# Hybrid MoBA and gated DeltaNet layer: softmax weights of seven heads transposed by DMA as 16-bit halves, their product with V moved to a slot of the delta branch

## The reference

```python
h = rms_norm(x, norm_gain)
aq, ak, av, az, bqkv, bz, bbeta, balpha, gate_a, gate_b = split(h @ w_in)
# branch A, per head; 256 tokens are one block, so attention is causal over all of them
lo = (q * dh**-0.5) @ k.T - slope * distance       # causal, -inf above the diagonal
p = softmax(lo)
ya = (p @ v) * silu(az)
# branch B, per head: causal convolution, then the chunked gated delta rule
tmat = triangular_solve(eye + lower, eye)
u, w = tmat @ vb, tmat @ (kb * exp(g))
out, state = scan over chunks
yb = rms_norm(out) * silu(bz)
merged = sigmoid(gate_a) * (ya @ w_branch_a) + sigmoid(gate_b) * (yb @ w_branch_b)
x = rms_norm(x + merged @ w_out)
```

## Time and profile before

| | |
|---|---|
| median of 3 runs | 771.9 us (771.65 to 772.05) |
| profiled execution, own time | 772.16 us |
| its span, first to last instruction | 770.4 us |
| mean granted clock of TensorE | 0.997 of 2.4 GHz |
| PE busy | 758.4 us (98%) |
| DVE busy | 564.8 us (73%) |
| ACT busy | 464.9 us (60%) |
| POOL busy | 122.1 us (16%) |
| DMA, share of 16 engines | 74.0% |

### The profile page before, as it was taken

How to read it: one execution, slowest core, us unless ns; L and a number is a source line. 1 busy time by engine, 2 the same in 40 slices (tenths; PEclk the granted TensorE clock), 3 DMA queues, 4 the chain that set the end, 5 groups by cost and what they waited for, 6 DMA issues and landing times.

```text
span 770.4 us, 10402 instructions
## 1 busy us (share of the span) xinstructions
PE 758.4 (98%) x3483; PEld 625.7 (81%) x3483; DVE 564.8 (73%) x1265; ACT 464.9 (60%) x697; POOL 122.1 (16%) x179
## 2 busy tenths in 40 slices
PE   8999999999999999999999999999999999999995
PEld 6888888888888888888888888888888888887884
DVE  5769847975895689479758956894798476966563
ACT  5686647656765675476657657764856663535441
POOL 6112011110101021101111120201021002512120
PEclk9999999999999999999999999999999999999998
DMA  9968767886788786778866786778676586798643
GB/s 254 241 170 219 205 163 214 193 217 179 184 209 198 192 208 181 199 192 197 212 174 203 200 217 170 203 188 215 174 213 182 181 222 182 217 331 268 190 153 109
DMA packets 225572, 154.44 MB, mean 200 GB/s; under 512 B 55408, under 2 KB 190576, under 8 KB 225392
## 3 DMA queue, kind: packets, MB, share of 16 engines
q1 hardware_dynamic: 225376, 153.53, 74.0%
q10 hardware_dynamic: 144, 0.26, 0.1%
HBM read 140.64 MB, written 2.11 MB: 185 GB/s over the span
## 4 chain that ended last, share of the span: by engine, by line
PE 95%; DMA 2%; issue 1%; DVE 1%; SPq 1%; ACT 0%; POOLq 0%; POOL 0%; DVEq 0%; ACTq 0%
PE pj L633 29%; PE pj L631 29%; PE pj L632 29%; DMA w_raw<-in_w_out_dram 1%; PE dn_ps L676 1%; PE pj L871 1%; PE pj L870 1%; PE pj L869 1%; DMA w_raw<-in_w_in_dram 1%; PE dn_ps L690 0%; PE dn_ps L685 0%; PE mo_ps L717 0%; PE dn_ps L677 0%; DVE w_lo L1169 0%; PE mo_ps L721 0%
## 5 line engine op out<-in xcount | busy, mean ns | idle before, releaser
L1169 DVE TENSOR_TENSOR w_lo<-w_raw,w_hi 128x1024 fp32r<-128x1024 f32 x251 | 312.6, 1250 | 138.1 <-ACT w_hi L885 137.1
L631 PE MATMUL pj<-w_hi,xt_hi 128*128 128x512 f32 x860 | 345.9, 402 | 1.2 <-DVE w_lo L1169 1.2
L633 PE MATMUL pj<-w_hi,xt_lo 128*128 128x512 f32 x860 | 336.6, 391 | 0.0
L632 PE MATMUL pj<-w_lo,xt_hi 128*128 128x512 f32 x860 | 335.8, 390 | 0.0
L885 ACT ACTIVATE w_hi<-w_raw 128x1024 fp32r<-128x1024 f32 x251 | 263.2, 1055 | 114.4 <-PE pj L633 88.3
L633 PEld LDWEIGHTS pj<-w_hi,xt_lo 128*128 128x128 f32 x860 | 161.4, 188 | 34.3
L631 PEld LDWEIGHTS pj<-w_hi,xt_hi 128*128 128x128 f32 x860 | 161.7, 188 | 33.5 <-issue 0.9
L632 PEld LDWEIGHTS pj<-w_lo,xt_hi 128*128 128x128 f32 x860 | 161.8, 188 | 31.4
L1356 DVE SCALAR_TENSOR_TENSOR xs<-lrep,xs 128x31 f32<-128x31 f32 (+30 forms) x496 | 88.9, 252 | 0.0
L550 POOL TENSOR_TENSOR xo<-v,own 128x128 f32<-128x128 f32 x16 | 13.6, 847 | 139.4 <-DVE v L1365 99.1
L1296 DVE SCALAR_TENSOR_TENSOR conv<-kk,hs,conv 128x255 f32<-128x255 f32 (+2 forms) x72 | 29.7, 480 | 0.0
(11 more groups left out here) (292 smaller groups left out, 760.6 us busy)
## 6 DMA issues: line engine op xcount, KB each, us to landing
w_raw<-in_w_in_dram SPq DMA_DIRECT2D x384, 256.0 KB, 3.3
w_raw<-in_w_out_dram SPq DMA_DIRECT2D x64, 256.0 KB, 4.0
w_raw<-in_w_branch_a_dram SPq DMA_DIRECT2D x32, 256.0 KB, 3.8
w_raw<-in_w_branch_b_dram SPq DMA_DIRECT2D x32, 256.0 KB, 3.7
gate<-in_x_dram SPq DMA_DIRECT2D x8, 256.0 KB, 5.2
gate<-in_x_dram SPq DMA_DIRECT2D x4, 512.0 KB, 7.7
gate<-in_final_norm_gain_dram SPq DMA_DIRECT2D x1, 1024.0 KB, 10.3
out_dram<-gate SPq DMA_DIRECT2D x4, 256.0 KB, 3.5
```

Source lines behind the costliest of these rows:

```text
L631: pe.matmul(bank[:, t, :], hi[:, k, tok], w_hi[:, slot, cs], start=(k == 0), stop=False)
L632: pe.matmul(bank[:, t, :], hi[:, k, tok], w_lo[:, slot, cs], start=False, stop=False)
L633: mm = pe.matmul(bank[:, t, :], lo[:, k, tok], w_hi[:, slot, cs], start=False, stop=(k == kt_all - 1))
L1169: dve.tensor_tensor(w_lo[:, slot, :], w_raw[:, slot, :], w_hi[:, slot, :].bitcast(F32), ALU.subtract).then_inc(lo_ready, 1)
```

## The change

For heads 0 to 6 the three PE transposes of `prob` and the copy from PSUM are gone. ACT makes `prob` into 16-bit halves (128x768) in slot 42, right behind the exponentials; SP issues one DMA transpose of them behind the loads of unit 3 of the next iteration (`J_P`); ACT joins the halves to `probT` at slot 47. The products with V move from slot 46 to slot 51, behind the delta branch's product; so does `ya` on DVE. `ya`'s halves move to slot 53, their DMA transpose from behind unit 6 to behind unit 9, the join from slot 53 to slot 60. One pair of semaphores now counts the transposes of `prob` and `ya`. Head 7 keeps its slots and its PE transposes.

```diff
-J_YA, J_DN, J_YB, J_MO, J_BACK = 6, 14, 16, 22, 23
+J_P, J_YA, J_YA_LAST, J_DN, J_YB, J_MO, J_BACK = 3, 9, 6, 14, 16, 22, 23
...
-M_NAT, M_HALVES, M_JOIN, M_QK, M_EXP, M_PT, M_PV, M_YA, M_YT = 31, 33, 39, 40, 42, 44, 46, 48, 53
+M_NAT, M_HALVES, M_JOIN, M_QK, M_EXP = 31, 33, 39, 40, 42
+def late_slots(h):
+    return (44, 46, 48, 53) if h == H - 1 else (47, 51, 53, 60)
+def pya_count(h):
+    return min(2 * h + 2, 2 * H - 1)
...
+        p_halves = halves[:, :, :].rearrange("p e n -> p (e n)")[:, 0:6 * P]
@@ sync, turned_behind
+                if h and j == J_P:
+                    sp.wait_ge(pya_halves, pya_count(h - 1) - 1)
+                    sp.dma_start_transpose(turned[:, 0:6, :], p_halves).then_inc(pya_landed, 16)
                 if h and j == J_YA:
-                    sp.wait_ge(ya_halves, h)
-                    turn_y(ya_landed)
+                    sp.wait_ge(pya_halves, pya_count(h - 1))
+                    turn_y(pya_landed)
@@ tensor, mo_step
-                if s == M_PT:
+                m_pt, m_pv, _, _ = late_slots(h)
+                if s == m_pt and h == H - 1:
                     pe.wait_ge(prob_ready, T * h + T)
                     for i in range(3):
                         mm = pe.transpose(C[:, i * P:(i + 1) * P], prob[:, i * P:(i + 1) * P], ident[:, :])
                     mm.then_inc(pt_done, 1)
-                if s == M_PV:
+                if s == m_pv:
                     pe.wait_ge(pt_ready, h + 1)
@@ tensor, between
                         if not first:
                             dn_step(s + SLOTS, h - 1)
+                            mo_step(s + SLOTS, h - 1)
@@ scalar, mo_step, at M_EXP
+                    if h < H - 1:
+                        act.wait_ge(prob_ready, T * h + T)
+                        act.activation(p_halves.rearrange("p (e n) -> p e n", e=2), halves_of(prob[:, :]),
+                                       ACT.Copy).then_inc(pya_halves, 1)
-                if s == M_PT:
-                    act.wait_ge(pt_done, h + 1)
+                m_pt, _, m_ya, m_yt = late_slots(h)
+                if s == m_pt and h < H - 1:
+                    act.wait_ge(pya_landed, 16 * (pya_count(h) - 1))
+                    joined(probT[:, :], turned[:, 0:6, :].rearrange("p (e b) n -> p e (b n)", e=2), pt_ready)
+                if s == m_pt and h == H - 1:
+                    act.wait_ge(pt_done, 1)
                     act.activation(probT[:, :], C[:, 0:3 * P], ACT.Copy).then_inc(pt_ready, 1)
@@ vector, mo_step: M_PV becomes m_pv (51), M_YT becomes m_yt (60)
-                        dve.wait_ge(ya_halves, h)
+                        dve.wait_ge(pya_halves, 2 * h)
```

More of the change, by code:

```diff
@@ L246, in build @@
         yb_hi_ready, yb_lo_ready = sem("yb_hi_ready"), sem("yb_lo_ready")
-        ya_halves, yb_halves, ya_landed, yb_landed = (sem(n) for n in ("ya_halves", "yb_halves", "ya_landed", "yb_landed"))
+        pya_halves, yb_halves, pya_landed, yb_landed = (sem(n) for n in (
+            "pya_halves", "yb_halves", "pya_landed", "yb_landed"))
         dn_halves_ready, mo_halves_ready, back_halves_ready = (sem(n) for n in (
@@ L393, in _ @@
                 load(w_a, c * CH, j, FIRST_A + n)
-                if n == J_YA:
-                    sp.wait_ge(ya_halves, H)
-                    turn_y(ya_landed)
+                if n == J_YA_LAST:
+                    sp.wait_ge(pya_halves, pya_count(H - 1))
+                    turn_y(pya_landed)
             for c in range(0, NC):
@@ L1007, in dn_step @@
                     act.wait_ge(yb_ready, T * h + T)
-                    act.wait_ge(ya_landed, 16 * h + 16)
+                    act.wait_ge(pya_landed, 16 * pya_count(h))
                     act.activation(halves[:, 0, :].rearrange("p (e n) -> p e n", e=2),
@@ L1050, in mo_step @@
                                    accum_out=mx[:, 3:4]).then_inc(prob_ready, 1)
-                if s == M_PT:
-                    act.wait_ge(pt_done, h + 1)
+                    if h < H - 1:
[8 more added lines that the diff above has]
+                    act.wait_ge(pt_done, 1)
                     act.activation(probT[:, :], C[:, 0:3 * P], ACT.Copy).then_inc(pt_ready, 1)
-                if s == M_YA:
+                if s == m_ya:
                     act.wait_ge(ya_ready, T * h + T)
@@ L1058, in mo_step @@
                     act.activation(halves[:, 0, :].rearrange("p (e n) -> p e n", e=2),
-                                   halves_of(ya[:, :, :].rearrange("p t n -> p (t n)")), ACT.Copy).then_inc(ya_halves, 1)
-                if s == M_YT:
-                    act.wait_ge(ya_landed, 16 * h + 16)
+                                   halves_of(ya[:, :, :].rearrange("p t n -> p (t n)")), ACT.Copy).then_inc(pya_halves, 1)
+                if s == m_yt:
+                    act.wait_ge(pya_landed, 16 * pya_count(h))
                     if not first:
@@ L1418, in mo_step @@
                     dve.reciprocal(mx[:, 6:8], mx[:, 2:4]).then_inc(rsum_ready, 1)
-                if s == M_PV:
+                _, m_pv, _, m_yt = late_slots(h)
+                if s == m_pv:
                     dve.wait_ge(pv_done, h + 1)
```

## The result

The changed kernel takes 777.06 us (median of 4 runs, 776.76 to 777.83), the kernel before 771.97 us beside it: a ratio of 1.0065 with a 95% interval of 1.0048 to 1.0082. It is 5.1 us slower; 778.8 was forecast. Its profiled execution took 777.83 us, 5.7 us over that of before, with a span of 776.1 us at a granted clock of 0.998.

A forecast was written before the change was run, and what follows sets the result against it. PE was taken to bound the kernel, with DVE's `xe` close behind. Six heads at 0.94 us (5.6 us), one late transpose at 1.2 us and nothing for heads 0 and 7 gave 6.8 us: 778.8 us, range 774.5 to 785.

The forecast's parts named there:

- The bound: PE bounds at 98% busy and 95% of the chain, but meets DVE's `xe` at slot 49 after gaining about 0.15 us.
- The room of some 0.15 us: Slot 49: what PE could gain before waiting, from the end of `xe` to its weight load, 0.16 us later.
- The place of the wait: PE waits for `xe` at the slot-49 product, L685, 1.27 us in each of heads 1 to 6.
- What is taken off PE: Ahead of slot 49 PE loses 0.99 us; 0.66 us of V returns at slot 51, saving 0.33 us a head.
- The halves on ACT: Slot 42: ACT's 0.84 us copy delays its split and DVE behind it, so `xe` ends 0.45 us later.
- The restart: Slot 49: PE loads weights right behind `xe` and starts L685 about 0.2 us after its end.
- The late transpose: Join at slot 47: one of heads 1 to 6 has its DMA transpose land at 5.1 us, costing 1.2 us.
- Heads 0 and 7: Head 0 gains 0.69 us and gives back 0.66 us, head 7 is unchanged: nothing for either.
- The transpose late in every head: Rival: the DMA transpose of `prob` lands at 5.1 us in each head, 13.0 us more, 784.9 us; chance 15%.
- The copy hides: Rival: ACT's slot-42 copy does not hold DVE, so only 2.8 us is lost, 774.7 us; chance 10%.
- The relief kept: Rival: `xe` moves earlier with PE, each head gains up to 0.33 us, 769.6 us; chance 8%.
- no change that can be told: Rival: a wait near 0.33 us at L685 and a time not told from before; chance 5%.

The follow-up runs named there:

- slots only: Changed kernel with the PE transposes kept and no DMA transpose of `prob`; products with V at slot 51, `ya` steps later: 774.15 us, 1.0027 of before.
- join at 48: Changed kernel with the join of `probT` at slot 48, behind the second evacuation of the gate columns: 776.49 us, 1.0060 of before.
- halves at 43: Kernel with the join at slot 48, plus ACT's halves of `prob` moved to slot 43, behind the split of unit 24: 773.74 us, 1.0026 of before.
- all later with slot 49: Kernel with the DMA path of `prob` behind both evacuations, delta products from `xe` on back at slot 49: 773.83 us, 1.0024 of before.
- all of it later: Changed kernel with halves at slot 46, join at 50, V at 52, `ya` steps later and delta products one slot later: 769.12 us, 0.9963 of before.
- the copy twice: Kernel with the join at slot 48, ACT's copy of `prob` to halves made twice, the second waiting for the first: 782.75 us, 1.0139 of before.
- V ahead: Changed kernel with the products with V (and `ya`) at slot 48, ahead of the slot-49 product: 772.72 us, 1.0007 of before.
- `xe` at slot 50: Kernel with the join at slot 48, plus every delta product from `xe` on one slot later: 772.52 us, 1.0004 of before.

## Why the prediction was right, point by point

**The bound.** That PE, at 98% and 95% of the chain, would meet DVE's `xe` as soon as it gained a little was right, and is shown from both sides: with `xe` at slot 49 every kernel in which PE comes early and V is behind waits there (changed, slots only, join at 48, halves at 43, all later with slot 49); with `xe` a slot later the kernel with all of it later is 4.7 us faster. The room of some 0.15 us was too small. It was measured to the weight load at 372.74; a held product starts 0.06 us behind `xe`, so it could come 0.33 us earlier than 372.97, of which 0.1 us is given back behind it.

**The place of the wait.** One wait of 1.27 us for `xe` was forecast. In head 5 PE waits 0.46 us for the first evacuation, 0.23 us for the second and 0.25 us for `xe`. By the starts, the three take 0.84 to 0.94 us in heads 1, 2, 4, 5 and 6. The step that the prediction left out is the first evacuation, which stands behind ACT's copy. Its time came out near because the waits stand in a row and the last one, for `xe`, sets when PE goes on.

**What is taken off PE.** Priced at 0.33 us a head; the kernel with all of it out of the way gains 0.43 us a head (71.11 to 70.68) and 2.9 us in seven. A fee for each stop between slots, which I took at nothing, is most of the difference. Behind the transposes the next large products come a little slower than 0.228 us: over nine steps, from 364.87 to 367.28, the stop costs 0.36 us and not 0.33. The shared slot saves as well: V and the delta product together cost 0.90 us over nine steps in the changed kernel, apart 0.69 and 0.26 us. That is 0.03 and 0.05 us of the 0.10.

**The halves on ACT.** Priced at 0.45 us of delay for `xe`; measured 0.46. The experiments with the copy later and the copy twice turn it off and double it.

**The restart.** I let the product start 0.2 us behind `xe`. It starts 0.06 us behind the end of `xe`. Some of it comes back behind it: from L685 to the second large product behind it took 373.42 - 372.97 = 0.45 us, and takes 448.55 - 447.99 = 0.56 us, 0.1 us more. From the slot-49 product to the slot-64 product a head takes 471.10 - 447.99 = 23.11 us, and took 466.47 - 444.10 = 22.37 us: 0.74 us and not the 0.66 us of V alone. From slot 64 to slot 49 it is 48.82 us against 48.76: 0.06 us where I had 0.28. The two mis-sized terms sum to 0.80 us in this head, and the heads without a late transpose run 0.75 us longer on average (71.86 us), where the prediction had 0.94. Over six heads that is 1.1 us of the 1.7 us by which the forecast was too high; the late transpose, below, is 0.3 us.

**The late transpose.** One in six was priced at 1.2 us; one came in the profiled execution, in head 3, and cost 72.76 - 71.86 = 0.9 us. That it was just one was luck: nothing in the rows of before said how many of the six would be late, and the executions without a profile do not show it. The place was right too: the join between the two evacuations. The unpriced wait for the first evacuation, 0.46 us in slot 48 of head 5, is free in the changed kernel, for PE would only wait longer for `xe` (all later with `xe` at slot 49, which has no evacuation wait, takes 71.48 us a head, and halves at slot 43, which has one, 71.47). In the kernels with V ahead and with `xe` at slot 50 it is what is left, and eats the gain of the transposes.

**Heads 0 and 7** cost nothing, as forecast: the slot-64 product of head 0 is at 110.91 and was at 110.89; from the slot-64 product of head 6 to that of head 7 it takes 614.08 - 542.97 = 71.11 us, and took 608.70 - 537.58 = 71.12.

**The rivals.** The transpose late in every head: refuted; where a join waited for it, the join began 3.6 us after the issue twice and 4.7 us once, and the other four joins found it there. The copy hides: refuted, for DVE waits 0.32 us for the split behind it and `xe` comes 0.46 us later. The relief kept, or no change that can be told: refuted as the change stands. The Trainium skill (Perfetto Trace Analysis, Identifying Performance Opportunities) says to optimize the most-contended engine first; the runs agree only once the dependent product has been moved, 769.12 us. The Trainium skill's advice to use TensorE for a 128x128 transpose whose result may go to PSUM (VectorE: DVE Perf Modes; it stands there under Rules for kernel authors, not under The three transpose paths) does not hold for this kernel where the round trip has cover: the kernel with DMA transposes and everything later is 2.9 us faster than before. How much of this the DMA path gives is not shown alone, since no kernel with PE transposes and all the later slots was run; 7 x 0.36 = 2.5 us is an estimate from the stop in slot 44.

## What to carry to other kernels

When work is taken off the engine that bounds, measure first how early its next operand is ready: here 0.16 us lay between the end of `xe` and the load of its weights, 0.39 us to its product, and nearly everything gained turned into a wait. Work moved from ahead of such a wait to behind it is paid twice, once as the wait and once in its new place (2.2 us in the kernel with the slots only); move the waiting instruction along with it, or leave filler ahead of it. An instruction put on an engine with room is not free where a chain passes through that engine's queue: look at what stands right behind it, above all copies that free a buffer for the bounding engine.

## What was not expected of the hardware

The DMA transposes of `turned`, which stand at the same places in every head, landed after 3.2 to 5.1 us in the kernel before; those of `prob`, all of one form, after 3.6 us twice and 4.7 us once where a join shows it. In head 7 of the kernel before with later delta products the join came 5.5 and 5.8 us behind the issue. A busy share of 98% on PE hid 0.94 us of waits in head 5; the chain and the starts of the large products showed them. And in head 5 of the changed kernel a product held for its operand started 0.06 us after the operand's writer ended, but the large products behind it ran 0.1 us late.
